# Three weight tiles interleaved behind each norm, the last square added by TensorE in PSUM, and unread matmuls on TensorE inside the norm's chain

## What is computed

```python
# first block, layers 0 and 1 (layer 0: attention, layer 1: gated delta rule)
h = rmsnorm(x, norm_mix_g) * (1 + scale_m) + shift_m
x = x + gate_m * mixer(h)
h = rmsnorm(x, norm_ffn_g) * (1 + scale_f) + shift_f
x = x + gate_f * ((silu(h @ w_gate) * (h @ w_up)) @ w_out)
x = rmsnorm(x, final_norm_g)
# second block, layers 0 and 1, on x and (until the last mixer) on the context
s = ffn_half_step(s); s = s + gate * (head_groups(...) @ w_out); s = ffn_half_step(s)
out = rmsnorm(x, final_norm_2)

def rmsnorm(x, g):
    return x * rsqrt(mean(x * x, axis=-1) + 1e-6) * g
```

## Time and profile before

| what | value |
|---|---|
| median of 3 runs | 2861.45 us (2860.23 to 2862.41) |
| time of the profiled execution | 2862.04 us |
| span of the profiled execution | 2860.2 us |
| TensorE matmul busy | 2579.6 us, 90% |
| VectorE busy | 1791.7 us, 63% |
| ScalarE busy | 1038.6 us, 36% |
| mean granted TensorE clock | 0.951 |
| DMA, mean | 142 GB/s |

### The profile page before, as it was taken

One profiled execution on the slowest core, in us unless ns is written; L12 is line 12 of the kernel. 1 busy time (PEld: TensorE's weight loads), 2 busy tenths in 40 slices (PEclk: granted clock), 3 DMA queues, 4 the chain that ended last, 5 costly groups with the idle time before them and its releaser, 6 DMA issues.

```text
span 2860.2 us, 37126 instructions
## 1 busy us (share of the span) xinstructions
PE 2579.6 (90%) x14954; PEld 2176.4 (76%) x14954; DVE 1791.7 (63%) x2952; ACT 1038.6 (36%) x1571; POOL 53.3 (2%) x56
## 2 busy tenths in 40 slices
PE   5888998876899889999897989999999999889998
PEld 4748998855799868888675568888778888766998
DVE  3647778644465677777745666666766565765655
ACT  4465435521254542222313442222332222434543
POOL 1000000020100000000000000000000000000000
PEclk9989999988999989999998999999999999899999
DMA  8776885522456646555312035555544444331563
GB/s 271 209 228 205 256 247 160 164 67 67 126 156 187 189 118 162 155 161 153 98 44 69 8 103 155 153 135 150 151 116 135 145 140 126 101 79 47 160 188 114
DMA packets 632561, 407.56 MB, mean 142 GB/s; under 512 B 27752, under 2 KB 588615, under 8 KB 631367
## 3 DMA queue, kind: packets, MB, share of 16 engines
q1 hardware_dynamic: 631712, 404.94, 49.1%
q10 hardware_dynamic: 678, 0.25, 0.0%
HBM read 404.09 MB, written 1.05 MB: 142 GB/s over the span
## 4 chain that ended last, share of the span: by engine, by line
PE 82%; DVE 9%; ACT 5%; DMA 2%; issue 1%; SPq 0%; ACTq 0%; POOL 0%; DVEq 0%
PE ps L1488 70%; DVE tmp L1924 1%; PE ps L1269 1%; PE ps L1498 1%; DVE h_lo L1916 1%; PE ps L1246 1%; DVE ada_acc L1733 1%; PE ps L789 1%; PE ps L526 1%; ACT w_hi L1607 1%; PE ps L797 1%; PE ps L799 1%; PE ps L1258 1%; ACT L1678 1%; DMA raw<-in_w_out 0%
## 5 line engine op out<-in xcount | busy, mean ns | idle before, releaser
L1488 PE MATMUL ps<-h_hi,w_hi 128*128 128x256 f32 (+1 forms) x3048 | 1018.5, 334 | 70.7 <-DVE h_lo L1916 60.1
L1607 ACT CAST w_hi<-raw 128x1024 fp32r<-128x1024 f32 (+3 forms) x557 | 555.0, 997 | 1383.1 <-PE ps L1488 1359.2
L1488 PE MATMUL ps<-h_hi,w_lo 128*128 128x256 f32 (+1 forms) x3048 | 1005.7, 330 | 0.0
L1488 PE MATMUL ps<-h_lo,w_hi 128*128 128x256 f32 (+1 forms) x3048 | 1005.4, 330 | 0.0
L1716 DVE TENSOR_TENSOR w_lo<-raw,w_hi 128x1024 fp32r<-128x1024 f32 (+3 forms) x557 | 645.0, 1158 | 351.8 <-ACT w_hi L1607 349.3
L1488 PEld LDWEIGHTS ps<-h_hi,w_hi 128*128 128x128 f32 x3048 | 587.1, 193 | 143.8 <-issue 68.1
L1488 PEld LDWEIGHTS ps<-h_lo,w_hi 128*128 128x128 f32 x3048 | 588.5, 193 | 50.2
L1488 PEld LDWEIGHTS ps<-h_hi,w_lo 128*128 128x128 f32 x3048 | 589.1, 193 | 47.0
L1488 PE MATMUL ps<-a_hi,w_hi 128*128 128x256 f32 (+1 forms) x1056 | 356.9, 338 | 0.1
L1488 PE MATMUL ps<-a_hi,w_lo 128*128 128x256 f32 (+1 forms) x1056 | 355.5, 337 | 0.0
L1488 PE MATMUL ps<-a_lo,w_hi 128*128 128x256 f32 (+1 forms) x1056 | 355.5, 337 | 0.0
(11 more groups left out here) (313 smaller groups left out, 1889.2 us busy)
## 6 DMA issues: line engine op xcount, KB each, us to landing
raw<-in_ffn_w_in SPq DMA_DIRECT2D x264, 512.0 KB, 4.5
ada_raw<-in_w_mod SPq DMA_DIRECT2D x120, 512.0 KB, 3.9
raw<-in_ffn_w_out SPq DMA_DIRECT2D x96, 512.0 KB, 4.5
ada_raw<-in_ada_w SPq DMA_DIRECT2D x40, 512.0 KB, 5.3
wide_rows<-in_ada_w SPq DMA_DIRECT2D x40, 512.0 KB, 4.8
raw<-in_ffn_w_out SPq DMA_DIRECT2D x48, 384.0 KB, 3.4
raw<-in_gdn_w_in SPq DMA_DIRECT2D x33, 512.0 KB, 4.1
raw<-in_w_in SPq DMA_DIRECT2D x26, 512.0 KB, 3.9
```

Source lines behind the costliest of these rows:

```text
L1488: last = mm(ps[0:m, slot, 0:n], w[:, slot, k * P:k * P + m], v[:, s0 + k, 0:n], start=(k == 0 and w is w_hi and v is hi), stop=(k == lin.k ...
L1607: nc.scalar.copy(w_hi[:, slot, 0:n], raw[:, slot, 0:n]).then_inc(s_hi, 1)
```

## The change

On TensorE the function `tile` becomes `tiles_together`. Behind a norm the first three tiles of the linear layer are multiplied together: for each feature block, the three matmuls of tile 0, of tile 1, of tile 2. The waits for `s_lo` and `s_evac` of a tile stand at its first block. All other tiles are as before. This holds for the first norm too.

The last square is no longer added on VectorE. `s_ssq` is raised after the second last, TensorE sums what there is, and then adds the last square with a second matmul into the same PSUM region. Between the two stand three matmuls of ones with the table `cos2` (float32, 256 columns) into bank 6, which nobody reads, and behind the second four more. This holds for every norm but the first. ScalarE computes a logarithm of one column (`table_seed`) in the last residual step, behind the cast of that step and ahead of the wait for the last block of x.

```diff
+TOGETHER = 3
-ADA_A, NORM_BANK = 4, 7
+ADA_A, WARM_BANK, NORM_BANK = 4, 6, 7
...
-            def tile(lin, j, h_waits):
...
+            def tiles_together(lin, js, h_waits):
...
                 for k in range(lin.kt):
                     if h_waits is not None:
                         pe.wait_ge(*h_waits(k))
...
+                    for j in js:
+                        g = lin.g0 + j
+                        slot = g % RING
+                        m = lin.columns(j)
+                        if k == 0:
+                            pe.wait_ge(s_lo, g + 1)
+                            if g >= RING:
+                                pe.wait_ge(s_evac, g - RING + 1)
+                        for w, v in ((w_hi, hi), (w_lo, hi), (w_hi, lo)):
+                            last = mm(ps[0:m, slot, 0:n], w[:, slot, k * P:k * P + m], v[:, s0 + k, 0:n],
+                                      start=(k == 0 and w is w_hi and v is hi), stop=(k == lin.kt - 1 and v is lo))
+                        if k == lin.kt - 1:
+                            last.then_inc(s_tile, 1)
...
-            def norm_sums(tokens, ready):
-
-                pe.wait_ge(s_ssq, ready)
-                mm(ps[:, NORM_BANK, 0:tokens], ones, ssq[:, 0:tokens], start=True, stop=True).then_inc(s_ssT, 1)
+            def keep_warm(n):
+
+                for _ in range(n):
+                    mm(ps[:, WARM_BANK, 0:T], ones, const("cos2"), start=True, stop=True)
+
+            def norm_sums(tokens, at_):
+
+                pe.wait_ge(s_ssq, at_["ssq"])
+                one = at_["n"] == 0
+                last = mm(ps[:, NORM_BANK, 0:tokens], ones, ssq[:, 0:tokens], start=True, stop=one)
+                if not one:
+                    keep_warm(3)
+                    pe.wait_ge(s_sq, at_["sq"])
+                    last = mm(ps[:, NORM_BANK, 0:at_["fresh"]], ones, sq[:, (KD - 1) % 2, 0:at_["fresh"]], start=False, stop=True)
+                last.then_inc(s_ssT, 1)
+                if not one:
+                    keep_warm(4)
...
             def linear(lin):
                 w = waits(lin)
+                i = next(n for n, s in enumerate(stages) if s is lin)
+                together = TOGETHER if not isinstance(stages[i - 1], Linear) and stages[i - 1][0] == "norm" else 1
+                tiles_together(lin, range(together), w)
                 for j in range(lin.n):
-                    tile(lin, j, w if j == 0 else None)
+                    if j >= together:
+                        tiles_together(lin, [j], None)
                     if lin.g0 + j in sum_at:
                         unit_sums(sum_at[lin.g0 + j])
...
                 elif lin.kind == "residual" and lin.more["last"]:
+                    if j == lin.n - 1:
+                        A(table_seed[:], const("eps"), ACT.Ln)
                     act.wait_ge(s_evac, g + 1)
                     A(sq[:, j % 2, 0:n], x[:, j, 0:n], ACT.Square).then_inc(s_sq, 1)
...
-                if k == KD - 1:
+                if k == KD - 2:
                     last.then_inc(s_ssq, 1)
...
-                    if squared:
-                        squares(st, KD - 1)
...
-                            if k == KD - 1:
+                            if k == KD - 2:
                                 last.then_inc(s_ssq, 1)
...
-                        add(KD - 1)
```

More of the change, by code:

```diff
@@ L273, in number @@
             n = KD * s[3] // T
-            stages[i] = ("norm", *s[1:], dict(n=norms, subs=subs, sq=sqs, ssq=ssqs, h=h_blocks))
+            stages[i] = ("norm", *s[1:], dict(n=norms, subs=subs, sq=sqs, ssq=ssqs, h=h_blocks, fresh=fresh))
             norms += 1
@@ L1486, in tile @@
                         pe.wait_ge(*h_waits(k))
-                    for w, v in ((w_hi, hi), (w_lo, hi), (w_hi, lo)):
-                        last = mm(ps[0:m, slot, 0:n], w[:, slot, k * P:k * P + m], v[:, s0 + k, 0:n],
-                                  start=(k == 0 and w is w_hi and v is hi), stop=(k == lin.kt - 1 and v is lo))
-                last.then_inc(s_tile, 1)
+                    for j in js:
[11 more added lines that the diff above has]
+                            last.then_inc(s_tile, 1)
             def unit_sums(unit):
```

16 lines of the change are left out of this document (7 added, 9 removed).

## The result

| what | before | changed |
|---|---|---|
| median | 2861.12 us (2859.02 to 2862.41, 6 runs) | 2873.46 us (2870.8 to 2879.8, 6 runs) |
| time of the profiled execution | 2862.04 us | 2873.81 us |
| its span | 2860.2 us | 2871.9 us |
| mean granted clock | 0.951 | 0.961 |

The ratio is 1.0046, 95% interval 1.0034 to 1.0059: slower by 12.3 us, where 2869.0 was forecast. Lines are those of the changed kernel here: the matmul of the linear layers is L1496, the modulation sums L1507, the first sum of a norm L1527, the unread matmuls L1521, the second sum L1531.

The account below looks back on a forecast made before the run. TensorE ends the chain last (82%), so gains come only from holes behind norms. Stages where TensorE stays last -11.1, where VectorE becomes last +17.7, final norm +0.9: +7.5 us on 2861.45 gives 2869.0 us, range 2856 to 2880.

Parts of the forecast that it names:

- chain of a T norm: In norms of 256 columns, the seed's table load moves onto the path between cast and square: logarithm 0.95 us later.
- stages where TensorE stays last: Two unhosted 256-column feed-forwards, both mixer projections and the layer 1 feed-forward of 512 columns: together -11.1 us.
- ffn1 0, to the first sum: 512-column feed-forward behind the replacing norm: first modulation sum waits for three VectorE pairs behind splits 4, 5, 6: +6.7 us.
- ffn2 0: 512-column feed-forward behind layer 0's mixer: modulation pairs queue on VectorE behind tile 0's later end: +1.4 us.
- delta projection: VectorE needs 3.08 us a tile against TensorE's 2.88 and starts its first convolution 3.8 us later: +2.7 us.
- first projection: TensorE stands still for `w_lo` of tiles 1 and 2, and later splits delay queued loads: +5.5 us (3.5 to 7).
- A: Rival: the clock stays high behind every norm, taking away 11.8 us: 2857.2 us; chance 0.17.
- B: Rival: VectorE does not become last, because pairs find room before tile 0 ends: 16.9 us less, 2852.1 us; chance 0.08.
- C: Rival: the clock falls in each norm as before, priced 2.5 to 3.4 us everywhere: +8 us, 2877; chance 0.12.
- D: Rival: the seed fails and the square brings a reload, two more 1.3 us loads in nine norms: 2890 us; chance 0.03.
- The rule on tables: Skill's rule: logarithm then exponential need one table load; could save 14 us in 11 norms; left out, 2855, chance 0.03.
- five signs of "right": Load between cast and square; 5 us first-projection idle; longer `ada_acc` waits; late delta-projection `w_lo` waits; mixer tile 3 earlier.

Follow-up runs that it names:

- seed ahead of the cast: Changed norm chain without three tiles together, seed in a free column of `rstd` and moved ahead of ScalarE's last weight cast, against the kernel before: 2880.4 us, ratio 1.0066.
- three tiles alone: Kernel before with only the three tiles behind every norm multiplied together, norm chain unchanged: 2864.3 us, ratio 1.0006.
- the run with the chain alone: Kernel before with only the changed norm chain (seed in `rstd`, last square added by TensorE, unread matmuls), tiles one by one: 2883.0 us, ratio 1.0070.
- the last run: Kernel before with the helpful parts together, 256-column layers 48 columns in, and three tiles with early rows in ffn1 0 and ffn2 0 too: 2813.2 us, ratio 0.9827.
- seed ahead of the cast, no unread: Changed norm chain, tiles one by one, seed moved ahead of the last cast, all seven unread matmuls removed, against the kernel before: 2857.5 us, ratio 0.9987.

## Why the prediction was right, point by point

| step | forecast, us | changed kernel, us |
|---|---|---|
| chain of a T norm | +0.95 | +0.9 |
| chain of a 2T norm | +1.15 | +1.1 |
| replacing norm, in all | +3.7 | +3.4 |
| stages where TensorE stays last | -11.1 | -10.5 |
| ffn1 0, to the first sum | +6.7 | +7.25, and 2 behind it |
| ffn2 0 | +1.4 | +3.8 |
| ffn 0 | +1.4 | +0.5 |
| delta projection | +2.7 | +3.8 |
| first projection | +5.5 | +3.7, less 1.1 in the attention |
| final norm | +0.9 | +1.1 |
| addresses | none | +8.9 and -9.3 |
| delta stage with the layer behind it, mixer stages | none | +2.3, -2.8 and +1.8 |

The first three rows are contained in the stages below them (where TensorE or VectorE is last). From the fourth row on the columns add up to +7.5 and, with a start 0.4 us later, to 11.8; the two spans differ by 11.7. Mis-sized were ffn1 0 (2.6 too cheap) and ffn2 0 (2.4), mostly for the low clock behind their new waits, 2 and 1.3 us: a wait of 7.45 us for a sum is a hole like that of a norm, and I had priced only the holes of norms. The delta projection was 1.1 too cheap, the delta stage (2.3) not in the sum at all, and the first projection 1.8 too dear (2.9 with the attention's -1.1, which is within what the attention does by itself); the idle 5 us between its first two blocks came as worked out (4.87), the loads behind them lost less. Since before's trace has one of the shortest first projections of the ten with single tiles (77.3 us, mean 78.9), even the +3.7 is in part that trace. So the mechanism was right, but that the total came within 5 us of the forecast is in part luck: errors of some 8 us too cheap met errors the other way, and the -2.8 and +1.8 of the mixer stages are no effect of the change.

**Chain.** The sizes were right. One reason was half right: in T norms I named the seed's load, and it was tied with the unread matmuls. With the seed ahead of the cast the four T chains kept 0.8 of 0.9, 0.5 of 1.2 and twice 0.5 of 0.9 us; without the unread matmuls as well the first stood at +0.1 and the others at -0.6. I had worked out TensorE's way for the 2T norm only. The same sum for T, 0.42 + 3 x 0.42 behind the start of the first sum at 240.69, gives 242.37 for the second sum, against a square that ends at 242.74: the two ways lie within 0.4 us. For 2T norms the run without them confirms the step, +1.1 to -0.2, and at the replacing norm +3.3 to +0.3:
```profile
1019.21 2.08 PE L1527 MATMUL ps<-ssq,consts 128*128 128x512 f32 x2 [6.99 <-DVE ssq L1967]
1021.08 2.77 PE L1521 MATMUL ps<-consts 128*128 128x256 f32 x6
1023.64 0.85 PE L1531 MATMUL ps<-sq,consts 128*128 128x256 f32 x2
```
There even the unread ones run at the low clock: the next matmul starts 2.56 us after the first of them, against 1.30 us in the 2T norm above.

**Clock.** Behind the 2T norm the stretches of the changed kernel are
```profile
1420.60:1426.00 5.40, 1.86 (x9) 1.29 (x7) 2.50 (x7) 4.30 (x7) 0.00 (x0) 1.00 0.00 0
1426.00:1430.10 4.10, 4.08 (x11) 3.25 (x12) 4.10 (x11) 2.66 (x6) 0.00 (x0) 0.61 0.02 4
```
The clock was up in the chain and fell just behind the first product. Tile 3 starts 18.1 us after it, 1.8 over three tiles at full pace; 2.2 was taken. In the T norm of ffn 0 it stayed up: 0.1, not 1.0. In the other three T norms tile 3 stands 1.6 us over the full pace, so there 1.0 was too little. Without unread matmuls (three tiles alone) the same 2T norm has 0.50 in the hole and 0.57 for 3.9 us behind the first product, so the unread ones lifted the clock where nobody multiplied and left the low stretch behind the product nearly as it was. Interleaved, three tiles took 18.1 and 18.0 us in ffn1 0 and ffn1 1 with unread matmuls and 19.2 without (three tiles alone), 18.1 and 18.0 in the mixer of layer 0, 11.8 and 11.8 in that of layer 1, 8.7 and 11.0 in ffn 0. But a difference of 1 us between two traces is chance in the 2T stages: over all traces with three tiles there (ffn1 and mixer of layer 0, ffn2 0, ffn1 1) it took 18.0 to 19.3 us with unread matmuls (eight cases, mean 18.4) and 17.8 to 19.3 without (twenty, mean 18.5). So behind 2T norms the clock they hold up is worth some 0.1 us. Behind T norms it is worth 2.2 to 2.5 us in ffn 0, 0.6 to 1.0 in the delta projection and ffn2 1, and nothing steady in ffn 1 (10.2 and 8.7 with, 10.0 to 10.3 without). Against that stand 0.9 to 1.2 us of chain each time, and 3.4 once. The four unread matmuls behind the second sum, which stand beside ScalarE's two steps, were only taken out together with the three ahead of it; whether those four alone would pay is not shown.

**TensorE last or VectorE last.** This division carried the forecast and is shown from both sides: three tiles in the five stages alone gave 14.4 us, and with the rows moved into VectorE's idle time the stages with rows turned from +7.0 to -2.8 and from +3.1 to -1.3. For the first projection and the delta projection no run put VectorE's work elsewhere; there it is argued from the trace, from the wait of 4.87 us for `w_lo` and from the tiles' pace.

**Rivals.** A (clock stays up everywhere) fell, by the 0.61 above; the Trainium skill ("TensorE: Matmul & The Clock Gate", section "Loop structure matters more than you think") is right here in that the pause ahead of the first product still cost the clock. Its worth was over-rated too: the run with the chain alone had less low clock than before, and was 21 us slower. B (VectorE does not become last) fell for this order, and holds once the rows stand at tile 0. C fell by size. D fell: the squares follow the seed with no load, 242.34 in the T norm. The rule on tables fell as well: in the changed kernel the logarithms and the exponentials still have 12 loads each, of 1.28 us. Of the five signs of "right" four appeared. The profile books no wait of TensorE for `w_lo` late in the delta projection, though its tiles went at VectorE's 3.08 us from tile 5 on, and at 2.88 in the kernel before.

## What to carry to other kernels

Work on the engine that waits is free only if nothing that someone else waits for stands behind it: unread matmuls ahead of a sum lengthened the chain by nearly their own time (1.1 of 1.3 us), and a clock kept up for a tile that goes at VectorE's pace buys nothing. Interleave tiles behind a barrier only where the engine that follows has no queue behind the first tile's end, or put that queue's independent work ahead of the instruction that waits. Ask of every late arrival what is the next late one, since two that are nearly tied give back their time only when both go.

## What the runs showed of the hardware

**The pace of a matmul follows where its columns lie.** Steps between starts at a clock of 1.00, by the address modulo 256 bytes in each partition at which the streamed tensor's columns begin (built, the kernel before has `h_hi` at byte 82048 of a partition and `a_hi` at 162880):

| address modulo 256 | 256 columns | 512 columns | seen in |
|---|---|---|---|
| 128 (`h` in before; `a` in the changed kernel) | 120 ns | 227 ns | all runs |
| 64 (`a` in before) | 113 ns, in one 256-column layer of each of three runs 118 | 233 ns | before and the eight runs with its addresses |
| 192 (16 columns in) | 118 ns | not run | two runs |
| 64 (48 columns in) | 113 or 118 ns | not run | the last run |

So at 64 there are two paces. At 48 columns in, ffn 1 begins at 113 ns and, after a tile with a stall in it, goes on at 118 for the next 158 us, so the address is not all. Each change between the two paces, here and in the single layers of the other runs, came with a step of 0.19 us or more between two starts, but most such steps changed nothing (the last layer of before has one of 0.31 us and stays at 113 ns). What the second factor is stays open, and so does whether 256 is the period. The Trainium skill ("SBUF — State Buffer", section "Specifications (TRN2)") names lines of 16 bytes as what costs an access; all addresses here are multiples of 64, so by it there would be no difference, and the measurement decides against that as the whole account. For a single matmul by itself the Trainium skill ("TensorE: Matmul & The Clock Gate", section "Back-to-back issue gap") has 2.5 ns over columns divided by 2.4 GHz, an estimate of 109 and 216 ns, and for a sustained stream of 512-column ones it gives 131 ns. All paces measured here are above both.

**The delta stage** took 213.0 to 214.3 us in all ten kernels without unread matmuls (before among them), and 216.8, 218.4, 220.0 and 220.8 in the four with them, though they stand outside it. Part of the difference arises where TensorE waits twice for the last rows of a modulation pair: 1.4 to 2.0 us together in the ten, 4.4 to 5.0 in the four. The first such wait without unread matmuls (seed ahead of the cast, no unread) and with them (seed ahead of the cast):
```profile
PE ps L530 <- DMA wide_rows<-in_w_mod: 1.0, 1, 1.0
```
```profile
PE ps L530 <- DMA wide_rows<-in_w_mod: 2.3, 1, 2.3
```
These waits are 3 us of the 7.1 between those two kernels; the rest is not accounted for. What moves the transfers is open, as no run aimed at it. In the changed kernel the stage is 2.5 us of the 12.3.
